# Splitting the first block's output product into three fp32r products, with its weights divided by ScalarE and GpSimd

## What is computed

```python
o_sb = stick_breaking_attention(q, k, v)                                 # 256 x 512
o_sb = rms_norm(o_sb, sb_out_norm)
state = state * w_t + (state a_t) b_t^T + v_t k_t^T ;  y_t = state r_t   # recurrence, 8 heads
yn = (y - mean) * rsqrt(var + LNX_EPS) * ln_w + ln_b
o_rw = (yn + bonus) * g                                                  # 256 x 512
x = x + concat([o_sb, o_rw]) @ w_out                                     # 256 x 1024 @ 1024 x 1024
x = x + 0.5 * swiglu(rms_norm(x, norm_ffn2), ...)                        # second feed-forward layer
```

## Time and profile before

| | |
|---|---|
| time of runs | median 1105.42 us (1105.32, 1105.42, 1107.82) |
| the profiled execution | 1107.49 us, its span 1105.7 us |
| TensorE busy | 1086.0 us (98%), mean granted clock 0.997 of 2.4 GHz |
| VectorE busy | 672.0 us (61%) |
| ScalarE busy | 448.1 us (41%) |
| GpSimd busy | 35.3 us (3%) |
| chain of work that ended last | TensorE 89%, VectorE 6%, ScalarE 3% |

### The profile page before, as it was taken

The page is one execution under the profiler, slowest core; times in us unless marked ns, Lnnn a source line. Parts: engine busy times, 40 slices in busy tenths (PEclk is TensorE's granted clock), DMA queues, the critical chain, the costliest instruction groups (busy, mean ns, idle before and its releaser), DMA issues.

```text
span 1105.7 us, 19149 instructions
## 1 busy us (share of the span) xinstructions
PE 1086.0 (98%) x8232; PEld 892.5 (81%) x8232; DVE 672.0 (61%) x848; ACT 448.1 (41%) x573; POOL 35.3 (3%) x30
## 2 busy tenths in 40 slices
PE   9999999999999999999999999999999999999997
PEld 8999999999988479999988999988999753434343
DVE  6488777789564856778766573277559542222123
ACT  6333334764542254333325242467583521211112
POOL 0000000000340000000003000000000000000000
PEclk9999999999999999999999999999999999999999
DMA  9976756454300349689862353332357979999994
GB/s 333 391 264 227 255 183 202 142 155 151 116 3 2 114 158 332 233 287 333 306 218 76 114 193 113 115 115 83 109 195 298 373 316 408 421 410 418 421 419 198
DMA packets 121012, 254.29 MB, mean 230 GB/s; under 512 B 6241, under 2 KB 91505, under 8 KB 109426
## 3 DMA queue, kind: packets, MB, share of 16 engines
q1 hardware_dynamic: 119890, 250.54, 62.1%
q10 hardware_dynamic: 1056, 2.79, 0.8%
HBM read 252.25 MB, written 1.06 MB: 229 GB/s over the span
## 4 chain that ended last, share of the span: by engine, by line
PE 89%; DVE 6%; ACT 3%; issue 1%; DMA 0%; SPq 0%; ACTq 0%; DVEq 0%
PE ps L827 54%; PE ps L774 33%; ACT arena L1612 2%; DVE ring_r L2179 1%; ACT arena_r L1612 1%; DVE ring_r L2312 1%; PE ps L1357 1%; DVE arena L2499 1%; DVE arena L2366 1%; DMA x<-in_x 0%; DVE arena L2381 0%; PE ps L795 0%; ACT gb_r L1612 0%; PE ps L1562 0%; PE ps L783 0%
## 5 line engine op out<-in xcount | busy, mean ns | idle before, releaser
L827 PE MATMUL ps<-hall_r,arena_r 128*128 128x256 f32 x1632 | 299.6, 281 | 0.0
L827 PE MATMUL ps<-arena_r 128*128 128x256 f32 (+1 forms) x1216 | 286.3, 325 | 0.0
L2179 DVE TENSOR_TENSOR ring_r<-ring,arena_r 128x2048 fp32r<-128x2048 f32 x88 | 203.1, 2312 | 109.4 <-ACT arena_r L1612 106.9
L827 PEld LDWEIGHTS ps<-hall_r,arena_r 128*128 128x128 f32 x1632 | 252.8, 188 | 1.2 <-issue 0.3
L1612 ACT ACTIVATE arena_r<-ring 128x2048 fp32r<-128x2048 f32 (+1 forms) x101 | 191.1, 1899 | 150.1 <-PE ps L827 139.8
L827 PE MATMUL ps<-hall_r,ring_r 128*128 128x256 f32 x816 | 227.8, 279 | 0.0
L827 PEld LDWEIGHTS ps<-arena_r 128*128 128x128 f32 x1216 | 203.9, 189 | 18.9 <-issue 0.7
L1612 ACT ACTIVATE arena<-ps 128x512 f32<-128x512 f32 (+3 forms) x136 | 80.4, 605 | 302.2 <-PE ps L827 188.0
L774 PE MATMUL ps<-arena 64*64 64x32 f32 (+7 forms) x1944 | 188.6, 321 | 4.1 <-ACT arena L1612 1.3
L774 PEld LDWEIGHTS ps<-arena 128*64 128x64 f32 (+3 forms) x1944 | 110.7, 143 | 64.8 <-issue 57.0
L827 PEld LDWEIGHTS ps<-hall_r,ring_r 128*128 128x128 f32 x816 | 154.9, 190 | 0.9
(11 more groups left out here) (274 smaller groups left out, 1144.2 us busy)
## 6 DMA issues: line engine op xcount, KB each, us to landing
ring<-in_w_in SPq DMA_DIRECT2D x35, 1024.0 KB, 5.2
arena<-in_w_exp_down SPq DMA_DIRECT2D x32, 1024.0 KB, 11.8
ring<-in_ffn_up SPq DMA_DIRECT2D x22, 1024.0 KB, 5.3
ring<-in_ffn_down SPq DMA_DIRECT2D x22, 1024.0 KB, 4.9
ring<-in_ffn_gate SPq DMA_DIRECT2D x21, 1024.0 KB, 6.5
arena<-in_w_mod SPq DMA_DIRECT2D x18, 1024.0 KB, 9.2
arena<-in_w_exp_up SPq DMA_DIRECT2D x16, 1024.0 KB, 14.5
ring<-in_w_exp_gate SPq DMA_DIRECT2D x16, 1024.0 KB, 11.4
```

Source lines behind the costliest of these rows:

```text
L827: m = pe.matmul(out_, w[i], h[j], start=start and i + j == 0, stop=stop and j == 1, skip_group_check=group)
L2179: tt(lo(n), slot(n), hi(n), ALU.subtract).then_inc(S("w_lo"), 1)
```

## The change

The output product is made as three fp32r products like the others (`mm3` in `out_rows`). `mix`, its left operand, moves to blocks 3 and 2; its high parts go to blocks 5 and 4, its low parts over `mix` itself. ScalarE copies the high part of one `w_out` piece in each round of the recurrence, ahead of `y_kept` (`out_weights_high`), into `wo_hi`, which is in turn arena block 25 with 26, the two halves of `hall`, and `gb`. GpSimd subtracts it from the weight in the ring slot (`lo(N_WOUT + c)`), one 128x2048 instruction for each piece. ScalarE and VectorE also split `mix` by quarters (`mix_high`, `mix_rest`). L2499 to L2501 become four quarters of 256 columns each, with a `mix_rest` between them. ScalarE's high parts of the next layer's first three weights now stand behind `mix_high(7)`, which needs the last quarter. SyncE's third load of modulation weights, which goes to `gb`, waits for the product.

```diff
--- before.py
+++ after.py
@@ -184,7 +184,7 @@
             "dve_once": [("first_lo", 2), ("mu_rest", 1), ("q_gain", 1), ("ctx_lo", 1), ("n4_lo", 1),
                          ("logits_kept_v", 1), ("picked_0", 1), ("rounds", 1),
                          ("gain_kept", 2), ("n6_gained", 3), ("n6_inv", 2)],
-            "dve_out": [("sb_out", 4), ("y_centred", 2), ("rw_out", 1)],
+            "dve_out": [("sb_out", 4), ("y_centred", 2), ("rw_out", 4)],
             "dve_tail": [("lam_prod", 1), ("head_gain", 1), ("y_four", 2), ("y_mix", 4),
                          ("route_w", 1), ("route_shift", 1), ("n5_inv", 2),
                          ("route_max", 1), ("chosen", 1), ("route_diff", 1), ("tables", 10), ("xn_lo", 1)],
@@ -440,7 +440,10 @@
         sb_b = A(5).rearrange("p (h k n) -> p h k n", h=2, k=4)
         z_a = ps[:, 2:6, :].rearrange("p (g h) (q n) -> p g h q n", g=2, q=2)
         z_b = ps[:, 0:2, :].rearrange("p h (k n) -> p h k n", k=4)
-        mix = [tiles(26), tiles(2)]
+        mix = [tiles(3), tiles(2)]
+        mix_hi, mix_lo = ([AR(j).rearrange("p (k n) -> p k n", k=4) for j in blks] for blks in ((5, 4), (3, 2)))
+        wo_hi = [AR(25, SLOT), hall_r[:, 0].rearrange("p k n -> p (k n)"), hall_r[:, 1].rearrange("p k n -> p (k n)"),
+                 gb_r[:, :, :].rearrange("p g n -> p (g n)")]
         inv_t, inv_tt, inv_x = (A(j).rearrange("p (i n) -> p i n", n=CH) for j in (23, 11, 15))
         def blocks_of(ap, level, odd):
 
@@ -560,6 +563,8 @@
                     sp.wait_ge(*W(tag + "_mod_step", per * (i - 3)))
                 elif tag == "f2" and i < 2:
                     sp.wait_ge(*W("rec_y", NCH))
+                elif tag == "f2" and i == 2:
+                    sp.wait_ge(*W("w_used", N_WOUT + 4))
                 elif tag == "f2" and i == 3:
                     sp.wait_ge(*W("ctx_turned", 4))
                 sp.dma_start(mod_stream[tag][i % 4].rearrange("p (k n) -> p k n", k=2),
@@ -749,6 +754,10 @@
             pool.wait_ge(*W("inv_x", 4))
             pool.memset(A(21), 0.0).then_inc(S("u_zero"), 1)
 
+            for c in range(4):
+                pool.wait_ge(*W("wo_hi", c + 1))
+                pool.tensor_tensor(lo(N_WOUT + c), slot(N_WOUT + c), wo_hi[c], ALU.subtract).then_inc(S("wo_lo"), 1)
+
             pool.wait_ge(*W("mod_kept", 3))
             pool.wait_ge(*W("gate_bias", 64))
             for j in range(4):
@@ -901,15 +910,17 @@
                         mod_sums(vec_, 1 + vec_ // 2)
                 down(FFC - 1)
 
-            def out_rows(n0, c, fs=range(2)):
-
-                weight(n0 + c)
+            def out_rows(c, fs=range(2)):
+
+                n = N_WOUT + c
+                pe.wait_ge(*W("wo_lo", c + 1))
+                w = [z.rearrange("p (k n) -> p k n", k=2) for z in (wo_hi[c], lo(n))]
                 for f, t, hs_ in last_first(c == 3, fs):
-                    lhs = mix[c // 2][:, 2 * (c % 2) + f, :]
+                    pe.wait_ge(*W("mix_lo", 2 * c + f + 1))
+                    heads_ = [z[c // 2][:, 2 * (c % 2) + f, t * P:(t + 1) * P] for z in (mix_hi, mix_lo)]
                     for h in hs_:
-                        m = mm(ps[:, 4 + 2 * t + h, :], lhs[:, t * P:(t + 1) * P],
-                               rows(n0 + c)[:, f, h * 512:(h + 1) * 512],
-                               start=c == 0 and f == 0, stop=c == 3 and f == 1, group=True)
+                        m = mm3(ps[:, 4 + 2 * t + h, :], heads_, [z[:, f, h * 512:(h + 1) * 512] for z in w],
+                                start=c == 0 and f == 0, stop=c == 3 and f == 1, group=True)
                     if c == 3 and (f, t + h) == (1, 1):
                         m.then_inc(S("row_part"), 1)
                 if f == 1:
@@ -1250,15 +1261,13 @@
             pe.wait_ge(*W("y_kept", 4))
             four(0, lambda o, k: mm(o, head_mean, y_rw[:, k, :]), "y_mean")
 
-            pe.wait_ge(*W("sb_out", 4))
-            out_rows(N_WOUT, 0, (0,))
+            out_rows(0, (0,))
             pe.wait_ge(*W("y_sq", 2))
             four(2, lambda o, k: mm(o, head_mean, sq[:, k, :]), "y_var")
-            out_rows(N_WOUT, 0, (1,))
-            out_rows(N_WOUT, 1)
-            pe.wait_ge(*W("rw_out", 1))
-            out_rows(N_WOUT, 2)
-            out_rows(N_WOUT, 3)
+            out_rows(0, (1,))
+            out_rows(1)
+            out_rows(2)
+            out_rows(3)
             pe.wait_ge(*W("y_root", 1))
             turn_apart("n3")
             ffn(N_FFN2, "f2")
@@ -1873,6 +1882,16 @@
             square_out(0)
             square_out(1)
             keep_sums(5)
+
+            def mix_high(k):
+                act.wait_ge(*(W("rw_out", k - 3) if k >= 4 else W("sb_out", k + 1)))
+                f(mix_hi[k // 4][:, k % 4, :], mix[k // 4][:, k % 4, :], ACT.Copy).then_inc(S("mix_hi"), 1)
+
+            def out_weights_high(c):
+                n = N_WOUT + c
+                act.wait_ge(*W(f"w_in_slot{n % RING}", 16 * (n // RING + 1)))
+                f(wo_hi[c], slot(n), ACT.Copy).then_inc(S("wo_hi"), 1)
+
             for c in range(NCH):
                 rows_ = slice((c % 2) * CH, (c % 2 + 1) * CH)
                 act.wait_ge(*W("rec_rhs", c + 1))
@@ -1882,14 +1901,20 @@
                     f(mix[0], banks(2), ACT.Copy).then_inc(S("sb_kept"), 1)
                     act.wait_ge(*W("sbo_ms", 2))
                     f(kn, banks(4), ACT.Sqrt, bias=EPS_COL).then_inc(S("sbo_root"), 1)
+                else:
+                    mix_high(c - 1)
+                out_weights_high(c)
                 act.wait_ge(*W("rec_y", c + 1))
                 f(y_rw[:, :, c * CH:(c + 1) * CH], ps[:, 2 + c % 2, 0:256].rearrange("p (k n) -> p k n", k=4),
                   ACT.Copy).then_inc(S("y_kept"), 1)
+            mix_high(3)
             for j in range(2):
                 act.wait_ge(*W("y_centred", j + 1))
                 f(sq[:, 2 * j:2 * j + 2, :], y_c[:, 2 * j:2 * j + 2, :], ACT.Square).then_inc(S("y_sq"), 1)
             act.wait_ge(*W("y_var", 2))
             f(y_n, banks(2), ACT.Sqrt, bias=LNX_COL).then_inc(S("y_root"), 1)
+            for k in range(4, 8):
+                mix_high(k)
             for t in range(TT):
                 act.dma_start(ctx_x[:, t, :], a["ctx_2"][t * P:(t + 1) * P, :]).then_inc(S(f"ctx_in{t}"), 16)
             for n in range(HI_RING):
@@ -2465,11 +2490,18 @@
                 stt(mix[0][:, k, :], mix[0][:, k, :], V("sb_out_norm", k), kn[:, k, :], ALU.mult,
                     ALU.mult).then_inc(S("sb_out"), 1)
 
+            def mix_rest(k):
+                v.wait_ge(*W("mix_hi", k + 1))
+                tt(mix_lo[k // 4][:, k % 4, :], mix[k // 4][:, k % 4, :], mix_hi[k // 4][:, k % 4, :],
+                   ALU.subtract).then_inc(S("mix_lo"), 1)
+
             for c in range(NCH):
                 rows_ = slice((c % 2) * CH, (c % 2 + 1) * CH)
                 v.wait_ge(*W("rec_u", c + 1))
                 v.wait_ge(*W("u_zero", 2))
                 v.tensor_copy(u_z[rows_, c % 2, :], ps[rows_, 1, :]).then_inc(S("u_kept"), 1)
+                if c:
+                    mix_rest(c - 1)
                 if c < NCH - 1:
                     v.wait_ge(*W("rec_state", c + 1))
                     sums = ps[:, 7, 0:256].rearrange("p (k n) -> p k n", k=4)
@@ -2486,6 +2518,7 @@
                 tt(y_c[:, 2 * j:2 * j + 2, :], y_rw[:, 2 * j:2 * j + 2, :],
                    ps[:, j, :].rearrange("p (f n) -> p f n", f=2), ALU.subtract).then_inc(S("y_centred"), 1)
 
+            mix_rest(3)
             for k in range(4):
                 m = ts(bonus[:, k, :], bonus[:, k, :], V("rw_ln_b", k), None, ALU.add)
             link(m)
@@ -2496,9 +2529,13 @@
                 m = stt(y_c[:, k, :], y_c[:, k, :], V("rw_ln_w", k), g_rw[:, k, :], ALU.mult, ALU.mult)
             link(m)
             v.wait_ge(*W("y_root", 1))
-            link(v.reciprocal(y_n, y_n))
-            link(tt(y_n, y_c, y_n, ALU.mult))
-            tt(mix[1], y_n, bonus, ALU.add).then_inc(S("rw_out"), 1)
+            for k in range(4):
+                link(v.reciprocal(y_n[:, k, :], y_n[:, k, :]))
+                link(tt(y_n[:, k, :], y_c[:, k, :], y_n[:, k, :], ALU.mult))
+                tt(mix[1][:, k, :], y_n[:, k, :], bonus[:, k, :], ALU.add).then_inc(S("rw_out"), 1)
+                if k:
+                    mix_rest(3 + k)
+            mix_rest(7)
             for n in range(HI_RING):
                 split(N_FFN2 + n)
             add_rows("x2_done", N_WOUT + 4, 1.0)
```

## The result

The changed kernel took **1119.41 us** (median of 4 runs, 1118.17 to 1120.61) beside 1106.04 for the kernel before (4 runs, 1105.32 to 1107.82): a ratio of 1.0118, 95% interval [1.0101, 1.0136]. The forecast was 1112.8 in [1106.5, 1117.0]. The forecast was set against a median of 1105.42 (three runs), so it stood for +7.4 us, where +13.4 came. The sign was right and the hold that it rested on is in the trace, but the time lies above the range.

A forecast was written before the change was run, and what follows sets the result against it. TensorE, busy nearly all the time, was taken as the bound. Later reciprocal 6.0, tail 0.4 and clock 0.95 gave +7.4 us: 1114.9 from the profiled 1107.49, 1112.8 against the median 1105.42; range 1106.5 to 1117.

The forecast's parts named there:

- the hold: In the recurrence, VectorE instructions with two SBUF operands wait until GpSimd's running one ends: 2.25, 2.8 and 2.2 us late.
- the clock in the recurrence: Rival: TensorE's clock also falls where it idles 2.3 and 2.8 us a round, 1.7 us more each, 1114.5 to 1116.2; chance 0.07.
- the place of the last hold: Round 3: GpSimd's last instruction holds the last `sb_out` product, due at 367.1, to 370.1, delaying the centring by 2.2 us.
- waits bounded at 1.7 us: Alternative for the three holds: each wait at most 1.7 us, giving 1.0, 1.0 and about 0.9 us; the whole wait was taken.
- T: Start of the first reciprocal behind the recurrence: forecast at 376.0, before at 369.99, so +6.0 us.
- The tail: From the first reciprocal to ScalarE's last root ahead of the next layer: 25.35 us, before 24.94, so 0.4 us longer.
- GpSimd's instruction: Each 2048-column subtraction of an output weight on GpSimd should take 3.82 us, estimated by one step of 0.91 per 512 columns.
- round 1's hold: L2480, the state's product, waits for GpSimd (348.1 to 351.9) and ends at 352.35: state 2.25 us late.
- the doubling: Rival: GpSimd takes twice as long for an fp32r output; rounds 1 and 2 lose about 6 each, some 1123; chance 0.05.
- the clock before the layer: TensorE idles over 6 us ahead of the transposes, so its clock falls and half of 16 run at half speed: 0.95 us.
- The way from the centring to T: On VectorE: centring 1.48, a quarter's subtraction 0.42, then L2490 to L2496 4.0 us, up to the first reciprocal.
- its own case: The forecast's main case, GpSimd holding VectorE, including bounded waits or GpSimd second in round 2: 1109.1 to 1114.5; chance 0.70.

The follow-up runs named there:

- write-only run: Changed kernel with GpSimd's four subtractions replaced by pairs of zero-writing memsets, the weights' low parts left out: 1107.08 us, ratio 1.0004.
- PSUM run: Changed kernel with the sum of the state written to a free PSUM bank, so its product has one SBUF operand: 1113.14 us, ratio 1.0059.
- run in pieces: Changed kernel with each 2048-column GpSimd subtraction issued as four instructions of 512 columns: 1108.87 us, ratio 1.0018.
- filling run: Changed kernel with five products of zeros on TensorE ahead of its wait for the state in rounds 2 and 3: 1114.58 us, ratio 1.0069.

## Why the prediction was low

Counted as the profiled execution, the forecast was 1114.9 and 1120.6 came: 5.7 us are missing. The steps that failed are the clock in the recurrence, held to be safe, and the place of the last hold; two terms were sized too small.

- **Right: the hold.** One row of 2.41 us in the trace before was read as "stands still until GpSimd's running instruction ends, unless an operand is in PSUM". The write-only run, the PSUM run and the run in pieces each bear out one clause of that. The Trainium skill ("SBUF — State Buffer", Who interferes with whom) has the same rule: a VectorE instruction with two SBUF inputs contends with a GpSimd instruction that reads SBUF and not with one that only writes it, and the second to issue is blocked until the first ends. The traces agree (3.93, 3.75 and 4.34 us). Holds of over 3 us also rule out waits bounded at 1.7 us.
- **Right: what costs nothing.** ScalarE's piece in round 1 ended at 347.75 and `y_kept` began at 349.16; a split product takes 0.70 us; the adds began at T + 20.56 (20.6 forecast); TensorE idled 6.7 us (over 6 forecast). The tail came to 0.3 where 0.4 stood.
- **Mis-sized: GpSimd's instruction**, 3.82 us by one step of 0.91 per 512 columns from plain fp32 rows, measured 4.51 to 4.59. It made round 1's hold 2.8 us instead of 2.25. In round 2 GpSimd led by 1.1 us and not 0.4, so the longer instruction still held only 2.6 (2.8 forecast). Together 5.4 for 5.05. With the clock at 1.00 (the filling run) the two are 2.9 and 3.2, so the size alone was worth 1.0 us here, and the slower clock hid part of it. Nothing in the trace before had 2048 columns or that output type, and the estimate had no upper end of its own but the doubling.
- **Wrong: the clock in the recurrence**, a rival at 0.07, cost 2.6 us. The argument was that gaps of 2.3 and 2.8 us are shorter than the 3.6 us of idling that left the clock at 1.00. The gaps were 2.64 and 2.44 us and it fell. That row came from the end of the program, behind unbroken work; in the recurrence TensorE had gaps every round already. One gap's length was the wrong thing to compare: the same 2.64 us behind the same work lowered the clock in this execution and left it at 1.00 in two others. What decides it stays open. The Trainium skill ("TensorE: Matmul & The Clock Gate", HAM oscillation — how this bites in real kernels) describes the pattern, bursts between stalls each of which starts cold again. This trace agrees in kind, and loses the clock at stalls shorter than those of the page's example.
- **Wrong: where the last hold falls.** The prediction let it meet `sb_out`'s product and priced it at 2.2 us; it met `mix_rest(2)`, which had been priced at nothing "in the gap between `u_kept` and the state". In round 3 there is no such gap, and the reciprocal and the product (2.2 us) stood queued behind it: 3.7 us. Most of the 1.45 us that this adds is the clock again: with the clock at 1.00 the same way takes 6.32 us, 0.95 less, and the other 0.5 is put down to GpSimd's longer instruction. TensorE's step was slow, so `u_kept` came late relative to GpSimd, which started 0.25 us behind it and not 1.5. With the clock held up by filling, the hold was where the prediction had put it. That run puts T 2.9 us earlier, which is the clock's whole price up to there (1.0 and 1.6 in the rounds, 0.95 here, less 0.6 that the second hold was shorter).
- **Mis-sized: the clock before the layer**, 0.95 us between bounds of 0 and 1.7, was 2.0. The prediction counted half of the transposes. The fall covered all of them and the first of the 48 products behind.
- The way from the centring to T took 5.67 us, forecast 5.9. The rest of the program gave 0.65 us more, which no run here explains.

These sum to 0.35 + 2.6 + 1.45 - 0.2 + 1.05 - 0.1 + 0.65 = 5.8. The first two large misses (2.6 and 1.45) belong together: a late engine makes TensorE idle, the clock falls, and the slower clock changes when VectorE next meets GpSimd, for the better in round 2 and for the worse in round 3. The third (1.05) is of another origin, since the clock also fell ahead of the layer in the runs without holds. The prediction added its terms as if they were independent, and the range's upper end (1117.0) took in the clock case and no combination of it with the others.

One figure of the prediction does not follow from its own terms: with waits bounded at 1.7 us the three sum to 2.9 us in place of 7.25, which gives 1108.4 and not 1109.1. It is only the lower end that the prediction names for its own case.

## What to carry to other kernels

Before giving GpSimd an elementwise instruction with two SBUF operands, list what VectorE must do during it: every instruction of VectorE with two SBUF operands in the critical chain can lose up to the whole of GpSimd's, so put the work where VectorE has none, or cut it into pieces (10.5 of 13.4 us came back that way). When a delay opens gaps on TensorE, price the lower clock together with the delay, as a range: here it fell after the same gap in one execution and not in two others. Shorter work on TensorE pays only once what follows is ready earlier too: here the saving of 5.6 us was worth nothing by itself and 4.6 us with the order of the splits changed.

## What was unexpected

- GpSimd took 4.53 us for 2048 columns where 1024 plain fp32 columns took 2.00, over twice as long; four pieces of 512 took 4.96 us together. Its memset of 2048 columns took 1.81. Which part of 4.53 the output type has was not measured.
- VectorE's reciprocal (one tensor operand) was never held: 1.74 us beside GpSimd in every trace read here. But in the run in pieces four TENSOR_SCALAR instructions took 2.15 us beside GpSimd's last piece, against 1.14 alone, so an instruction with one tensor operand can be touched too. The Trainium skill ("SBUF — State Buffer", Who interferes with whom) names `tensor_scalar` among those that can take both ports; no run was made to settle it.
- Zero products made the kernel faster by 3.0 and 4.8 us, though they add work to the engine that is busy 97% of the span.
